# GpSimd norms the first 512 columns of the last token block, and the last norm's row scale comes from a logarithm and an exponential

## The reference, cut to what matters

```python
LN_EPS = 1e-5

def layer_norm(x, g, b):
    xf = x.astype(jnp.float32)
    mu = xf.mean(-1, keepdims=True)
    var = jnp.square(xf - mu).mean(-1, keepdims=True)
    return ((xf - mu) * lax.rsqrt(var + LN_EPS) * g + b).astype(x.dtype)

# in the second block, for each of its two layers:
y = mixed @ w_out[i]
h = layer_norm(DEEPNORM_ALPHA * h + y, ln_g[i], ln_b[i])
```

## Time and profile before

| | us |
|---|---|
| median of 3 runs | 1998.5 (1997.56 to 1998.78) |
| the profiled execution, its time | 1997.84 |
| its span in the trace | 1996.1 |
| TensorE busy | 1979.1 |
| VectorE busy | 1248.1 |
| ScalarE busy | 872.7 |
| GpSimd busy | 15.7 |

### The profile page before, as it was taken

How to read it: one execution, slowest core, us unless ns; L and a number is a source line. 1 busy time by engine, 2 the same in 40 slices (tenths; PEclk the granted TensorE clock), 3 DMA queues, 4 the chain that set the end, 5 groups by cost and what they waited for, 6 DMA issues and landing times.

```text
span 1996.1 us, 24439 instructions
## 1 busy us (share of the span) xinstructions
PE 1979.1 (99%) x10596; PEld 1698.8 (85%) x10596; DVE 1248.1 (63%) x1142; ACT 872.7 (44%) x826; POOL 15.7 (1%) x53
## 2 busy tenths in 40 slices
PE   8999999999999999999999999999999999999997
PEld 7888888888888888888888888888988888888886
DVE  6766666656666664466666446657866754566665
ACT  7544545445443443344444345343433534344532
POOL 1000000000000000000000000000000000000000
PEclk9999999999999999999999999999999999999999
DMA  9654554776656555656565756755595656644652
GB/s 344 192 185 148 169 169 141 237 260 219 195 172 204 175 191 189 208 182 200 174 205 171 276 186 212 227 163 169 184 335 179 224 190 190 190 148 148 208 193 85
DMA packets 294541, 391.11 MB, mean 196 GB/s; under 512 B 6305, under 2 KB 225185, under 8 KB 292641
## 3 DMA queue, kind: packets, MB, share of 16 engines
q1 hardware_dynamic: 291984, 365.41, 56.5%
q0 software_dynamic: 2304, 24.12, 3.0%
q10 hardware_dynamic: 144, 0.01, 0.0%
HBM read 381.12 MB, written 8.39 MB: 195 GB/s over the span
## 4 chain that ended last, share of the span: by engine, by line
PE 99%; DVE 0%; DMA 0%; ACT 0%; DVEq 0%; issue 0%
PE G L443 40%; PE G L447 20%; PE G L490 11%; PE G L492 11%; PE G L491 11%; PE SB L785 1%; PE OB L806 1%; PE G L512 0%; PE G L510 0%; PE G L511 0%; PE OB L809 0%; PE SB L682 0%; PE G L485 0%; PE G L486 0%; PE G L484 0%; PE TB L1093 0%
## 5 line engine op out<-in xcount | busy, mean ns | idle before, releaser
L368 DVE TENSOR_TENSOR hl_ring<-raw,hl_ring 128x2048 fp32r<-128x2048 f32 x344 | 774.8, 2255 | 506.6 <-ACT hl_ring L365 505.9
L365 ACT ACTIVATE hl_ring<-raw 128x2048 fp32r<-128x2048 f32 x344 | 647.5, 1885 | 577.4 <-PE G L492 313.5
L443 PE MATMUL G<-ahl,hl_ring 128*128 128x512 f32 x2112 | 666.5, 397 | 6.9 <-DVE hl_ring L390 6.9
L447 PEld LDWEIGHTS G<-ahl,hl_ring 128*128 128x128 f32 x2112 | 397.6, 188 | 94.0
L447 PE MATMUL G<-ahl,hl_ring 128*128 128x256 f32 x2112 | 416.2, 278 | 0.0
L443 PE MATMUL G<-ops,hl_ring 128*128 128x512 f32 x1216 | 384.3, 397 | 0.0
L443 PEld LDWEIGHTS G<-ahl,hl_ring 128*128 128x128 f32 x2112 | 322.9, 189 | 7.3 <-DVE ahl L404 6.9
L447 PEld LDWEIGHTS G<-ops,hl_ring 128*128 128x128 f32 x1216 | 228.5, 188 | 54.0
L447 PE MATMUL G<-ops,hl_ring 128*128 128x256 f32 x1216 | 239.3, 278 | 0.0
L443 PEld LDWEIGHTS G<-ops,hl_ring 128*128 128x128 f32 x1216 | 185.6, 189 | 0.3
L490 PE MATMUL G<-hl_ring,hhl 128*128 128x512 f32 x352 | 137.0, 389 | 0.0
(11 more groups left out here) (347 smaller groups left out, 1701.7 us busy)
## 6 DMA issues: line engine op xcount, KB each, us to landing
raw<-in_w_in SPq DMA_DIRECT2D x116, 1024.0 KB, 5.4
raw<-in_w_out SPq DMA_DIRECT2D x48, 1024.0 KB, 5.2
raw<-in_w_ffn_gate SPq DMA_DIRECT2D x44, 1024.0 KB, 5.1
raw<-in_w_ffn_up SPq DMA_DIRECT2D x44, 1024.0 KB, 5.1
raw<-in_w_ffn_down SPq DMA_DIRECT2D x40, 1024.0 KB, 5.1
raw<-in_w_kv_shared SPq DMA_DIRECT2D x24, 1024.0 KB, 5.2
raw<-in_w_mem_kv SPq DMA_DIRECT2D x16, 1024.0 KB, 5.3
ahl<-memop_scratch POOLq DMA_DIRECT2D x2, 4096.0 KB, 14.3
```

The lines of the kernel that those rows point to most:

```text
L365: eng.activation(hi[:, s, 0:size], raw[:, r, 0:size], ACT.Copy).then_inc(hi_ready, 1)
L368: eng.tensor_tensor(lo[:, s, 0:size], raw[:, r, 0:size], hi[:, s, 0:size].bitcast(F32), ALU.subtract).then_inc(lo_ready, 1)
L443: eng.matmul(G[:, 2 * pair + b, :], hi[:, s, w], p.rhs(k), start=first and q == 0, stop=False)
L447: last = eng.matmul(G[:, 2 * pair + b, 0:TOK], lo[:, s, w], p.rhs(k)[:, 0, :], start=False, stop=final and q == len(ks) - 1)
```

## The change

For token block 1, columns 0 to 511 (`AIDED`) are taken from VectorE and given to GpSimd, which does three instructions on them: (x - mean) times the row scale, times gain, plus bias. VectorE's pass over the gain covers 1536 columns there, and its three last instructions cover 768, 512 and 256 columns. For block 0 the ranges stay. ScalarE no longer takes the root: it computes the logarithm of variance plus epsilon, waits for it, and takes the exponential of -0.5 times that, so `lnrs` holds the reciprocal root and VectorE's reciprocal goes, in both blocks. SP stores `AIDED` of block 1 as a transfer of its own, after the first and before the second of VectorE's parts, and waits for GpSimd's third instruction there.

```diff
-        PARTS = (slice(0, 1024), slice(1024, 1536), slice(1536, 2048))
+        PARTS = ((slice(0, 1024), slice(1024, 1536), slice(1536, 2048)),
+                 (slice(512, 1280), slice(1280, 1792), slice(1792, 2048)))
+        OWN = (slice(0, 2048), slice(512, 2048))
+        AIDED = slice(0, 512)
...
             for t in range(TT):
-                for i, w in enumerate(PARTS):
-                    sp.wait_ge(l_out, len(PARTS) * t + i + 1)
+                for i, w in enumerate(PARTS[t]):
+                    if t == 1 and i == 1:
+                        sp.wait_ge(l_aided, 3)
+                        sp.dma_start(A["result"][P:2 * P, AIDED], xt[:, 1, AIDED]).then_inc(out_stored, 16)
+                    sp.wait_ge(l_out, 3 * t + i + 1)
                     sp.dma_start(A["result"][t * P:(t + 1) * P, w], xt[:, t, w]).then_inc(out_stored, 16)
-            sp.wait_ge(out_stored, TT * len(PARTS) * 16)
+            sp.wait_ge(out_stored, 7 * 16)
...
             pool.wait_ge(rows_loaded, 32)
+            pool.wait_ge(t_agg, 4)
+            pool.wait_ge(l_rstd, 2)
+            own = xt[:, 1, AIDED]
+            pool.tensor_scalar(own, own, lnmv[:, 1, 0:1], lnrs[:, 1:2], ALU.subtract, ALU.mult).then_inc(l_aided, 1)
+            pool.wait_ge(l_aided, 1)
+            pool.tensor_tensor(own, own, lnrow[:, 0, AIDED], ALU.mult).then_inc(l_aided, 1)
+            pool.wait_ge(l_aided, 2)
+            pool.tensor_tensor(own, own, lnrow[:, 1, AIDED], ALU.add).then_inc(l_aided, 1)
...
             for t in range(TT):
                 act.wait_ge(t_agg, 3 + t)
-                act.activation(lnrs[:, t:t + 1], lnmv[:, t, 1:2], ACT.Sqrt, bias=epsl[:, 0:1]).then_inc(l_rstd, 1)
+                act.activation(lnrs[:, t:t + 1], lnmv[:, t, 1:2], ACT.Ln, bias=epsl[:, 0:1]).then_inc(l_ln, 1)
+                act.wait_ge(l_ln, t + 1)
+                act.activation(lnrs[:, t:t + 1], lnrs[:, t:t + 1], ACT.Exp, scale=-0.5).then_inc(l_rstd, 1)
...
                     dve.wait_ge(rows_loaded, 32)
-                    dve.scalar_tensor_tensor(xt[:, t, :], xt[:, t, :], lnmv[:, t, 0:1], lnrow[:, 0, :],
+                    own = OWN[t]
+                    dve.scalar_tensor_tensor(xt[:, t, own], xt[:, t, own], lnmv[:, t, 0:1], lnrow[:, 0, own],
                                              ALU.subtract, ALU.mult).then_inc(l_y, 1)
                     dve.wait_ge(l_rstd, t + 1)
-                    link(l_nm, dve.reciprocal(lnrs[:, t:t + 1], lnrs[:, t:t + 1]))
                     dve.wait_ge(l_y, t + 1)
-                    for w in PARTS:
+                    for w in PARTS[t]:
                         dve.scalar_tensor_tensor(xt[:, t, w], xt[:, t, w], lnrs[:, t:t + 1], lnrow[:, 1, w],
                                                  ALU.mult, ALU.add).then_inc(l_out, 1)
```

More of the change, by code:

```diff
@@ L219, in program @@
         q_ready = sem("q_ready")
-        l_rstd, l_nm, l_y, rows_loaded = sem("l_rstd"), sem("l_nm"), sem("l_y"), sem("rows_loaded")
-        l_out, first_rows = sem("l_out"), sem("first_rows")
+        l_rstd, l_ln, l_y, rows_loaded = sem("l_rstd"), sem("l_ln"), sem("l_y"), sem("rows_loaded")
+        l_out, first_rows, l_aided = sem("l_out"), sem("first_rows"), sem("l_aided")
         q_scaled = sem("q_scaled")
```

## The result

The changed kernel takes 2001.57 us (median of 22 runs, 2001.12 to 2002.17), the kernel before 1997.87 us (22 runs, 1997.20 to 1998.81): a ratio of 1.0018, 95% interval 1.0013 to 1.0024. It is 3.7 us slower: 0.18%, though the interval reaches beyond 0.2%. The profiled execution took 2001.64 us with a span of 1999.9.

The account below looks back on a forecast made before the run. TensorE's matmuls bound 99% of the chain, leaving a 10.0 us tail. GpSimd's start 1989.8 + 3.34 + 1.62 = 1994.76, span end 1998.24, 2.1 us later: 1998.5 + 2.1 = 2000.6 us, range 1997.4 to 2002.4.

Parts of the forecast that it names:

- part 1: VectorE after the last matmul: 512 columns fewer save 0.54 us in each of two passes; reciprocal goes, 0.03 gap stays.
- part 2: ScalarE's logarithm, table load and exponential: 1.92 us to the consumer, all but 0.09 covered by VectorE's gain pass.
- Rival E: ScalarE's new sequence doesn't fit under VectorE's gain pass: some 1.4 us more than the forecast, 2002.0 us; chance 0.05.
- part 3: GpSimd's three 512-column instructions: 1.08 us each, 3.34 us with two handovers, bounds 1.7 and 5.0.
- part 4: GpSimd beside VectorE's last pass: the engines exclude each other while VectorE streams, 1.62 us; bounds 0 and 2.07.
- part 5: SP's stores: three, 0.655 MB, go out behind GpSimd's end; the span ends 3.48 us after it.
- the handovers: Gaps between GpSimd's three linked instructions: two of 0.05 us.
- Rival B: GpSimd runs unhindered beside VectorE's last pass: +0.5 us, 1999.0 us; chance 0.28.
- C: GpSimd near the memset's rate and unhindered, ending ahead of VectorE: -0.8 us, 1997.7 us; chance 0.12.
- D: GpSimd at the cast's rate, excluded for each VectorE instruction's full length: +4.3 us, 2002.8 us; chance 0.05.

Follow-up runs that it names:

- p1_ln_exp: The kernel before with only logarithm and exponential in place of root and reciprocal, no GpSimd work: 1998.22 us against 1998.22, ratio 1.0.
- e1_behind: The changed kernel with GpSimd waiting for VectorE's last instruction before its first; ran once: span 2000.3 us, tail 14.48.
- e2_psum: The changed kernel with VectorE's three last instructions on block 1 taking their second tensor from PSUM; ran once: span 1998.5 us, tail 12.30.
- e6_256: The changed kernel with 256 instead of 512 columns on GpSimd; ran once: span 1997.0 us, tail 10.67.
- e7_one_piece: The changed kernel with VectorE's last pass of block 1 as one 1536-column instruction, GpSimd's columns stored behind it; ran once: span 1998.9 us, tail 12.68.
- e5_store_last: The changed kernel with GpSimd's 512 columns stored last: 2000.58 us, ratio to before 1.0012.
- v2_psum256: Against the kernel before: 256 columns on GpSimd, stored last, bias row copied to PSUM for VectorE's last pass on block 1: 1997.60 us, ratio 0.9997.
- p2_gpsimd: The changed kernel with root and reciprocal back, so GpSimd's columns alone: 2001.40 us against 1998.22 before, ratio 1.0017.

## Why the prediction was right in direction and too small in size

The forecast was 2000.6 us, 2.1 above before; 2001.57 was measured, 3.7 above, inside the range. That the time itself is off by only 1.0 us is partly luck: the forecast stands on a median before of 1998.5 from three runs, and 22 runs gave 1997.87. The change was 1.6 us larger than forecast. The mechanism, GpSimd on the path, held off by VectorE, with stores behind it, is the forecast one. By its steps, in the profiled execution:

- **VectorE's share** (part 1): 1.82 us for 1536 columns against 1.81 expected. A small step failed: I put the gap that stays without the reciprocal at 0.03 us, and it is 0.11, against 0.12 with it; alone the removal brought nothing (p1_ln_exp).
- **ScalarE's sequence** (part 2): 1988.05 to VectorE's start at 1989.97 is 1.92 us, as read from lines 642 and 644. The next function came 1.30 us behind the start of the load (1988.36 to 1989.66). The drain that the Trainium skill ("ScalarE: Activation LUTs", section "What ACT_TABLE_LOAD costs") adds didn't appear. There was a load before each of the two functions in both blocks, four in all, with one of them on the path. Rival E is out.
- **GpSimd's own time** (part 3): the mis-sized term. 3 by 1.08 us was 3.24; by themselves they take 2.08 + 1.26 + 1.26 = 4.60 (e1_behind). The two-input ones lie near my value. The first is outside my bounds: 2.08 us against an upper end of 1.64 from the cast. I had taken all three for one kind; the one with row operands and two operations is another, and no row of before stood near it.
- **Exclusion** (part 4): that VectorE's two inputs in SBUF hold GpSimd back is right, and shown by e2_psum. GpSimd lost 1.30 us against 1.62. VectorE lost another 0.35 us, which isn't on the path; the sum, 1.65, is near my 1.62 for VectorE's streaming, but it was 1.61 in e6_256 too, where VectorE streams 256 columns more, so that rule isn't shown. In the kernel before, the quick 128x6 instruction that spoke against it began at 8.78, ahead of VectorE's at 8.86, and the slow one at 9.06, behind it. The order of starts could account for both, as it could for who paid in e6_256; that is an inference. The condition that the Trainium skill gives ("SBUF — State Buffer", section "Who interferes with whom"), two SBUF inputs of VectorE, is borne out. Full blocking of the later one, which that section words for VectorE's two-port modes and I took for this case, fits GpSimd behind VectorE (e7_one_piece), but not VectorE behind GpSimd: 0.18 us of stretch in 1.06 us side by side (e6_256), and a 256-column instruction that ended in the middle of GpSimd's (changed kernel).
- **Stores** (part 5): 3.76 us from GpSimd's end to the end of the span against 3.48: the 0.655 MB took 2.0 us instead of 1.75. e5_store_last shows that stores queued behind the wait count, by their issues (0.86 us) more than by their bytes (0.35).

The sum of the misses: +1.00 for the first GpSimd instruction, +0.36 for the other two, -0.32 for the exclusion, +0.28 behind GpSimd's end, +0.06 for the handovers (0.08 each instead of 0.05), +0.06 for GpSimd's later start: 1.44 us, which is 13.62 minus 10.04 minus the expected 2.14.

Rival B, GpSimd unhindered, fell: the changed kernel's first instruction was held for 1.30 us, and e2_psum, which is what B describes, still has a tail 2.3 us longer than before, not 0.5, because of GpSimd's own times. C fell with GpSimd's own times. D asked for 4.8 us of GpSimd's time and full exclusion; 4.6 us and 1.3 came, so the result, 3.7 us, stands closer to D (4.3 us) than to the forecast (2.1), and 0.05 was too little for it.

## What to carry to other kernels

Before work is handed to GpSimd in a tail, its own duration there has to be measured, form by form. Beside VectorE instructions with two inputs in SBUF some 1.6 us were lost here between the two engines, in changing shares; with one input in SBUF nothing was. Even then the versions with GpSimd were no faster than the one that only cut VectorE's work and the stores differently. A wait put in the middle of a store queue holds back every store behind it: what is ready last should be stored last, and several small stores that are ready at once cost their issues one after the other. An instruction removed from a chain that waits for its own results may bring nothing, because the gap stays.

## What the runs showed of the hardware

- GpSimd on 128 partitions of float32, unhindered: two-tensor product or sum 1.26 us for 512 columns and 0.72 for 256 (2.1 ns a column and 0.2 us fixed); tensor with two per-row operands 2.08 and 1.22 (3.4 ns a column, 0.4 fixed); with one 1.57; with two fixed numbers 1.94. I had not expected the one-tensor forms to be slower than the two-tensor one.
- Reading the second tensor from PSUM costs VectorE nothing (472 ns against 475) and frees GpSimd (2.08 us instead of 3.38). The copy into PSUM is extra work, 0.58 us for 512 columns in v2_psum256, done while ScalarE was idle.
- With two SBUF inputs the loss of both engines together was 1.57 to 1.65 us in four kernels (changed, p2_gpsimd, e6_256, e7_one_piece). In the three where VectorE's pass began 0.11 to 0.18 us ahead, GpSimd bore 1.2 to 1.6 us of it; in e6_256, where GpSimd began 0.16 us ahead and had half the columns, VectorE bore 1.1.
- SP takes 0.33 us for a store issued by itself. Issued one behind the other, stores begin 0.38 and then 0.48 us apart (1996.16, 1996.54, 1997.02 in the changed kernel).
